# The two score products of differential attention, issued next to each other

## The reference

```python
def diff_attention(q, k, v, lq1, lk1, lq2, lk2, subln_g, rel_bias, lam_init):
    q = q.reshape(B, S, DA_HEADS, 2, DA_HEAD_DIM) * (DA_HEAD_DIM ** -0.5)
    ...
    def block(args):
        ...
        logits = jnp.einsum('bqhmd,bkhmd->bhmqk', qb, k).astype(f32) + bias
        logits = jnp.where(dist >= 0, logits, NEG_INF_2)
        p = jax.nn.softmax(logits, axis=-1)
        attn = p[:, :, 0] - lam * p[:, :, 1]
        return jnp.einsum('bhqk,bkhe->bqhe', attn.astype(v.dtype), v)
```

## Time and profile before

| what | value |
| --- | --- |
| median of three runs | 3623.53 us |
| span of the profiled execution, first to last instruction | 3609.5 us |
| median less span | 14.0 us |
| TensorE matmuls busy | 3463.7 us, 96% |
| VectorE busy | 1597.8 us, 44% |
| ScalarE busy | 698.1 us, 19% |
| GpSimd busy | 2346.8 us, 65% |
| mean granted TensorE clock | 0.951 |
| first attention stage of `diff()` | from 2065.2 us |
| second attention stage of `diff()` | from 3080.0 us |

### The profile page before, as it was taken

One profiled execution on the slowest core, in us unless ns is written; L12 is line 12 of the kernel. 1 busy time (PEld: TensorE's weight loads), 2 busy tenths in 40 slices (PEclk: granted clock), 3 DMA queues, 4 the chain that ended last, 5 costly groups with the idle time before them and its releaser, 6 DMA issues.

```text
span 3609.5 us, 41977 instructions
## 1 busy us (share of the span) xinstructions
PE 3463.7 (96%) x14430; PEld 2654.1 (74%) x14430; DVE 1597.8 (44%) x1864; ACT 698.1 (19%) x1380; POOL 2346.8 (65%) x1046
## 2 busy tenths in 40 slices
PE   8999899989988999989999999999999999999998
PEld 6756688868556888768888758888888887578886
DVE  4554311134555111165524856552355338665532
ACT  2242211022342110031101232110111102221110
POOL 6602577757204777748877707887788777258874
PEclk9997899989988999989999969999999999699999
DMA  4200122222101222212223202222222232112221
GB/s 161 76 1 24 65 94 95 96 83 88 36 1 53 93 93 94 95 57 93 93 94 108 88 12 88 93 93 94 94 93 93 93 108 88 35 65 93 93 93 64
DMA packets 82012, 286.31 MB, mean 79 GB/s; under 512 B 9531, under 2 KB 13020, under 8 KB 81628
## 3 DMA queue, kind: packets, MB, share of 16 engines
q1 hardware_dynamic: 76032, 275.81, 22.7%
q10 hardware_dynamic: 5852, 8.78, 0.7%
HBM read 280.89 MB, written 3.67 MB: 79 GB/s over the span
## 4 chain that ended last, share of the span: by engine, by line
PE 69%; DVE 4%; issue 2%; ACT 1%; DVEq 0%; ACTq 0%
PE bank_v L329 13%; PE bank_v L330 13%; PE bank_v L331 13%; PE bank_a L329 7%; PE bank_a L330 7%; PE bank_a L331 7%; PE bank_s L551 2%; PE bank_v L463 2%; PE bank_a L439 1%; PE bank_s L368 1%; PE bank_s L553 1%; PE bank_s L376 1%; DVE lru_x L1439 0%; DVE lru_x L1446 0%; PE bank_s L476 0%
## 5 line engine op out<-in xcount | busy, mean ns | idle before, releaser
L301 POOL TENSOR_TENSOR w_hi<-raw,zero 128x1024 fp32r<-128x1024 f32 x520 | 996.1, 1916 | 1186.5 <-PE bank_v L331 930.1
L304 POOL TENSOR_TENSOR w_lo<-raw,w_hi 128x1024 fp32r<-128x1024 f32 x520 | 1350.8, 2598 | 40.8
L329 PE MATMUL bank_v<-xn_hi,w_hi 128*128 128x512 f32 x1408 | 565.5, 402 | 13.5 <-DVE xn_lo L1024 13.4
L329 PE MATMUL bank_a<-xn_hi,w_hi 128*128 128x512 f32 x1360 | 544.3, 400 | 23.7 <-DVE xn_lo L1086 15.1
L330 PE MATMUL bank_v<-xn_lo,w_hi 128*128 128x512 f32 x1408 | 559.3, 397 | 0.0
L331 PE MATMUL bank_v<-xn_hi,w_lo 128*128 128x512 f32 x1408 | 559.1, 397 | 0.0
L330 PE MATMUL bank_a<-xn_lo,w_hi 128*128 128x512 f32 x1360 | 540.1, 397 | 0.0
L331 PE MATMUL bank_a<-xn_hi,w_lo 128*128 128x512 f32 x1360 | 540.0, 397 | 0.0
L331 PE MATMUL bank_v<-h_hi,w_lo 128*128 128x512 f32 x1056 | 417.7, 396 | 0.0
L329 PE MATMUL bank_v<-h_hi,w_hi 128*128 128x512 f32 x1056 | 417.6, 396 | 0.0
L330 PE MATMUL bank_v<-h_lo,w_hi 128*128 128x512 f32 x1056 | 417.6, 396 | 0.0
(11 more groups left out here) (290 smaller groups left out, 3707.9 us busy)
## 6 DMA issues: line engine op xcount, KB each, us to landing
raw<-in_w_stream SPq DMA_DIRECT2D x520, 512.0 KB, 3.3
rope<-in_rope ACTq DMA_DIRECT2D x2, 1024.0 KB, 6.0
da_v<-t_rows ACTq DMA_DIRECT2D x2, 1024.0 KB, 6.1
out<-resid SPq DMA_DIRECT2D x4, 512.0 KB, 2.6
t_rows<-t_row ACTq DMA_DIRECT2D x1, 1536.0 KB, 6.9
resid<-in_x SPq DMA_DIRECT2D x4, 256.0 KB, 3.8
resid<-in_x ACTq DMA_DIRECT2D x4, 256.0 KB, 9.1
mla_v<-in_alibi ACTq DMA_DIRECT2D x2, 512.0 KB, 6.9
```

Of the source, the lines that this page charges most:

```text
L301: pool.tensor_tensor(w_hi[:, u, :], raw[:, u, :], zero[:, 0:1].to_broadcast([P, UNIT]), ALU.add).then_inc(*hi_split.done(("unit", u)))
L304: pool.tensor_tensor(w_lo[:, u, :], raw[:, u, :], w_hi[:, u, :].bitcast(F32), ALU.subtract).then_inc(*w_split.done(("unit", u)))
L329: pe.matmul(out, lhs_hi, rhs_hi, start=first, stop=False)
```

## The change

Both score banks are taken first. Then the score matmuls of map 0 and map 1 are issued one behind the other, and after them the four bias matmuls, map 0's two and map 1's two. The increment of `scores_ready` stays with the last bias matmul of each map. Nothing else changes.

```diff
                     lo = max(i - 1, 0) * P
-                    for m in range(2):
-                        key = ("diff", h, i, m)
-                        b = s_bank(key)
+                    banks = [s_bank(("diff", h, i, m)) for m in range(2)]
+                    for m, b in enumerate(banks):
                         pe.matmul(b[:, 0:n], mix2[half(m), h, cut], da_k[half(m), h, 0:n], start=True, stop=True)
+                    for m, b in enumerate(banks):
 
                         pe.matmul(b[:, lo:n], ident_r[:, :], t5_hi[:, 2 * h + m, 256 - (n - lo):256],
                                   start=False, stop=True, skip_group_check=True)
                         pe.matmul(b[:, lo:n], ident_r[:, :], t5_lo[:, 2 * h + m, 256 - (n - lo):256],
                                   start=False, stop=True, skip_group_check=True
-                                  ).then_inc(*scores_ready.done(key))
+                                  ).then_inc(*scores_ready.done(("diff", h, i, m)))
```

## The result

The changed kernel takes 3566.82 us, the median of four runs from 3562.91 to 3571.23. The kernel before took 3623.82 beside it (four runs, 3623.15 to 3628.16). The ratio is 0.9845, interval 0.9834 to 0.9857, so 57 us are saved. The forecast was 3604 us, with a range down to 3583: the sign was right, the size was three times too small, and the result lies outside the range.

What follows compares the result with a forecast made beforehand. PE's own sequence was taken as the bound, DVE under half full. Savings of 9.93 us less 0.36 give 9.6 per round, 19 in two: 3623.5 - 19 = 3604 us, own range 3599 to 3609, wider range 3583 to 3618.

Steps and rivals of the forecast that it cites:

- rival 3: Score pairs of the attention stages: full overlap, a pair costs one score; 40 us saved, 3584 us; chance 0.07.
- (a): Score and bias matmuls: one of two round trips between array shapes goes, 0.30 us per item at the lower clock.
- rival 1: Score pairs: halves do not run together, only shape changes and one load saved; 9.6 us, 3614 us; chance 0.15.
- (b): Neighbouring scores: score 0's last pass overlaps score 1's first, three passes for four; half a score saved, 1.00 us at 512.
- (c): Both waits for score banks stand before the first score; only n = 2 is hurt, starting 0.36 us later.
- (d): Map 0 is complete later, map 1 earlier; DVE gets two reductions in a row, covered by its slack; price 0.
- Rival 4: Attention heads: denser work lifts the clock for one more 512 wide item each; another 17 us, 3587 us; chance 0.09.
- rival 2: Score pairs: no overlap at all, not even the load, only (a) left; 5.9 us, 3618 us; chance 0.13.
- rival 5: Upper clock lost in the stretches behind the values; beside rival 2, 13 us more than before, 3637 us; chance 0.07.
- median less span: Whole kernel: the median of the runs lies 14.0 us above the profiled span, kept unchanged in the forecast.

Runs made afterwards that it cites:

- neighbours without overlap: Changed kernel with both score products made from map 0's half of the partitions, so they can't run together: 3610.83 us, ratio 0.9965.
- the doubled products: Changed kernel with both score products issued twice, in order 0, 1, 0, 1 or 0, 0, 1, 1: 3571.13 and 3577.83 us.
- filled kernel before: Kernel before with 18 added full-row matmuls ahead of n = 2 and three ahead of the squared sums in steps 9 and 13: 3584.06 us.

## Why the prediction was wrong

Right were the place (the two attention stages), the sign, the price of an overlapped pair as rival 3 worked it out, and that PE's own sequence bounded the kernel before. The steps in turn:

**(a) The shape.** Forecast 0.30 per item at the lower clock. It measured 0.61 at 512, and 6.3 and 6.5 per stage for neighbours without overlap, where rival 1 had 4.8. The rows had held it: half of the way in and out was hidden in the price of the product, where I called it a load. Two slips beside it move nothing: rival 1's terms add up to 4.7, and the third stretch at the upper clock of a round was 10.2 us long, not 6.9.

**(b) The overlap. This is the step that failed first.** "PE starts its matmuls in order, and the passes of one score share rows and follow each other", so three passes for four. The pair takes 2.01 us, one product, and the doubled products show that each half takes its own next pass, past work of the other half. The sentence that gave rival 3 only 0.07 ("an engine that starts in order") rested on no row. With nothing in the trace on the question, the two ends should have had like chances. The Trainium skill's packing rule, cited there, spoke for rival 3. By itself this makes 40 us of the forecast 19, 3584 us. Beside it the clock rose, which my sum left as it was.

**Rival 4, the clock, chance 0.09.** It came too, and its place was nearly right: scores of 512 at the upper level. It was sized at 17 us. The filled kernel before shows that a raised clock can bring 39. I had carried only one more item per head to the upper clock, where 85 us of lower-clock time went. The rule of the Trainium skill ("TensorE: Matmul & The Clock Gate", Part 1) that activity releases the throttle agrees with the rise, but the row of 10.00 us busy in 10.00 at 0.50 (and the 13.60 of 13.60 in the earlier trace rows) shows PE busy with the clock down.

**The rivals were not exclusive.** I gave rivals 3 and 4 separate chances, though in these two stages one change brings both: with the two products at work at once the pair is shorter, and the clock is up more. Their sum, 40 + 17, happens to be the measured 57. That is no confirmation. The clock alone is worth 39 and the neighbours alone 12, but a saved pass is worth only half as much at the upper clock as at the lower, and 13 us of new waits come on top, so the parts can't be summed.

**(c) The common wait.** The 0.36 is seen, but an own wait gains nothing either, as said above. PE's wait at n = 2 grew from 4.12 us to 5.82: PE arrives 1.4 us earlier and is released 0.3 later.

**(d) "DVE is far ahead", price 0.** It was mis-sized. PE's idle time grew by 13.4 us over both stages, by the list under the result: the exponentials at n = 2 and n = 5, the squares (0.66 to 1.47), the last transposes. A head of 13.71 us holds 11.51 of DVE, where 20.60 held 9.24, but seven of its 32 instructions are left over from the items before. The next head, from 2103.89 to 2116.80, holds 8.98 in 12.91, and DVE itself waits for PE there. So DVE is much nearer than it was, and does not set the pace alone. I had said that waits for ACT in front of the scores in many items would mean that my theory fails outright. They came in two of sixteen; what refuted the theory was the price of the pair, 2.01 us. The warning of the Trainium skill ("TensorEngine Tiling (Array Packing)", PSUM Bottleneck), which I put aside, came nearer than my price of nothing: DVE, which reads the scores out of PSUM, is now busy 52.0 of 70.7 us.

**Rivals 1, 2 and 5** are out: there is overlap, the change does what it says, and the clock was gained. **The median less span** was 1.8 us and not 14.0; since I kept it unchanged, it cost the sum nothing.

What stays open: which activity sets the clock. In the kernel before it stood up for stretches of 6.9 us, in the filled one the same order of products kept it up for 57 us, and no run separates how it is held from how it is raised. How much of the 57 us is the overlap's own cannot be given as one number either: 18 us are left beside the clock's 39, and some of them are the saved changes of shape. Nor is the 39 exactly the clock's share in the change, which had more time at the lower level left than the filled kernel.

## What to carry to other kernels

Matmuls that use half of the array's rows belong next to each other, in pairs on different halves, and the pair is to be priced as one: here two float32 products took 2.01 us where one took 2.00. In a stage at the lower clock, ask first what would raise it, since a few idle microseconds filled with useless full-row matmuls were worth 39 us here. The pairing alone is no recipe for the clock: in `stick` it came with a fall. And price the waits for the other engines against the shortened stage, not against the old one: here 13 us of the work that PE lost came back as waits that had been priced at nothing.

## What the hardware did that I had not expected

- A product on one half of the rows can start ahead of an earlier one on the other: in the order 0, 0, 1, 1 all four passes of the two first copies started before the second copies, in pairs 13 to 14 ns apart.
- A change between the 64 row and the 128 row shape costs 0.17 and 0.13 us inside the product at the lower clock, beside the steps of the biases, 0.61 for a round trip. I had seen half of it.
- Adding 24 matmuls to each stage of the kernel before made the kernel 39 us shorter.
- The clock stayed at 0.50 while PE was busy 10.00 of 10.00 us with both products on one half and the matmuls between them. It rose in the same stage when both halves worked, and yet fell from 0.82 to 0.69 in `stick` when its products were paired.
- The same kernel had 0.90 or 0.82 of the clock in one 180 us stretch of the first block, in different executions, the largest part of 20 us between two spans with no edit.
